# Sample columns of the expert outputs from gathered rows, and the last group in token halves

## The reference, cut to what matters

```
qh = (xb @ w_pq).reshape(..., 8 heads, 2, 128)
s = qh . sub_keys                             # 128 scores for each half and head
sv, si = top_k(s, 16)                         # of each half
cand = sv[half 0][:, None] + sv[half 1][None, :];  top_s, pos = top_k(cand, 16)
eid = si[half 0] * 128 + si[half 1]           # at pos: 16 of 16384 experts for each head
gate = softmax(top_s)
act = gelu(u_experts[eid] . xb)
out = sum over the 8 * 16 (gate * act) * v_experts[eid]
x = x + out;   y = rmsnorm(x) * norm_final
```

## Time and profile before

| | |
|---|---|
| median of 3 runs | 5116.29 us |
| profiled execution | 5119.69 us, span 5117.5 us |
| TensorE / VectorE / ScalarE / GpSimd busy | 98% / 48% / 24% / 24% |
| mean granted TensorE clock | 0.988 of 2.4 GHz |
| HBM traffic | 539 MB read, 111 MB written, 127 GB/s |

### The profile page before, as it was taken

How to read it: one execution, slowest core, us unless ns; L and a number is a source line. 1 busy time by engine, 2 the same in 40 slices (tenths; PEclk the granted TensorE clock), 3 DMA queues, 4 the chain that set the end, 5 groups by cost and what they waited for, 6 DMA issues and landing times. The chain is left out here.

```text
span 5117.5 us, 92582 instructions
## 1 busy us (share of the span) xinstructions
PE 5005.5 (98%) x39028; PEld 4930.2 (96%) x39028; DVE 2452.4 (48%) x3709; ACT 1231.9 (24%) x1251; POOL 1206.5 (24%) x522
## 2 busy tenths in 40 slices
PE   8999999999989999999999999999999999999997
PEld 8999888899969999999999999999999999999997
DVE  4455556533222335765777776501444444444443
ACT  4233334222121222222111111122212212212212
POOL 0000000020001003333333333334223233233232
PEclk9999999899989999999999999999999999999998
DMA  3233433232342234333444344443333333333332
GB/s 150 96 130 119 153 105 108 93 121 90 132 149 86 95 108 164 120 120 106 137 132 150 133 153 137 153 165 144 135 138 128 135 135 129 138 131 129 141 125 76
DMA packets 233944, 651.28 MB, mean 127 GB/s; under 512 B 13696, under 2 KB 126720, under 8 KB 177024
## 3 DMA queue, kind: packets, MB, share of 16 engines
q1 hardware_dynamic: 233856, 650.03, 36.0%
HBM read 539.42 MB, written 110.56 MB: 127 GB/s over the span
## 5 line engine op out<-in xcount | busy, mean ns | idle before, releaser
L237 PE MATMUL pu<-xhi,whi 128*128 128x272 f32 x7456 | 1548.0, 289 | 28.6 <-DVE xlo L503 12.5
L237 PE MATMUL pu<-xhi,wlo 128*128 128x272 f32 x7456 | 1545.9, 289 | 0.0
L237 PE MATMUL pu<-xlo,whi 128*128 128x272 f32 x7456 | 1540.7, 288 | 0.0
L237 PEld LDWEIGHTS pu<-xhi,whi 128*128 128x128 f32 x7456 | 1174.4, 189 | 31.5 <-issue 24.3
L237 PEld LDWEIGHTS pu<-xlo,whi 128*128 128x128 f32 x7456 | 1175.2, 189 | 0.0
L237 PEld LDWEIGHTS pu<-xhi,wlo 128*128 128x128 f32 x7456 | 1167.2, 189 | 0.0
L221 ACT CAST whi<-raw 128x2048 fp32r<-128x2048 f32 x393 | 748.5, 1905 | 1593.3 <-PE pm L237 1183.5
L226 POOL TENSOR_TENSOR wlo<-raw,whi 128x2048 fp32r<-128x2048 f32 x128 | 601.5, 4699 | 1210.1 <-ACT whi L221 1210.1
L226 DVE TENSOR_TENSOR wlo<-raw,whi 128x2048 fp32r<-128x2048 f32 x265 | 609.4, 2300 | 390.9 <-ACT whi L221 383.9
L1492 POOL TENSOR_TENSOR clo<-coef,chi 128x544 fp32r<-128x544 f32 x124 | 261.6, 2130 | 994.3 <-ACT chi L1496 994.3
L1556 DVE TENSOR_TENSOR x<-pm,x 128x544 f32<-128x544 f32 x256 | 185.5, 724 | 584.1 <-PE pm L237 584.1
(11 more groups left out here) (298 smaller groups left out, 4796.4 us busy)
## 6 DMA issues: line engine op xcount, KB each, us to landing
raw<-units SPq DMA_DIRECT2D x393, 1024.0 KB, 4.9
h_s<-h_out SPq DMA_DIRECT2D x128, 272.0 KB, 2.1
gate_s<-table SPq DMA_DIRECT2D x17, 2048.0 KB, 9.4
h_in<-h_s SPq DMA_DIRECT2D x32, 1088.0 KB, 7.1
gate_in<-gate_s SPq DMA_DIRECT2D x32, 1088.0 KB, 9.1
q_s<-q_out SPq DMA_DIRECT2D x32, 320.0 KB, 2.2
x<-xT SPq DMA_DIRECT2D x8, 1088.0 KB, 6.7
qh<-q_s SPq DMA_DIRECT2D x8, 1088.0 KB, 7.3
```

Of the source, the lines that this page charges most:

```text
L237: ins = nc.tensor.matmul(out, w, xs[b][m == 1], start=(first and n == 0 and m == 0), stop=(last and n == len(terms) - 1 and m == 2))
```

## The change

- **Sample tokens.** The output stage no longer carries the 32 sample columns: `chi`, `clo`, `coef`, `h_in`, `gate_in` and the table have 512 columns (`TP`), and a product has one operand of 512 columns in one bank instead of two of 272. The table has 16 chunks; the transposes and copies of the fifth token block go.
- **Slots.** In the fifth block the 96 empty tokens become three copies of the 32 sample tokens (`again`), so that its 128 partitions hold each token four times. Partition group g keeps 32 of the token's 128 slots (`dve_keep_slots`): a gate, the address of the h value in `h_s`, and the address of the expert's weight row in `units`.
- **Gathers.** In the output stage GpSimd issues for each of the 32 slots one indirect DMA for 128 values of h and 16 for 128 rows of 512 bytes (`pool_rows`), behind the coefficient steps of `pair_pool`: one slot in a group, two in groups 0, 6, 12, 18 and 24, done by group 26. Three buffers. Two groups later VectorE multiplies h by the gate and adds h * gate * row to `row_sum` (`dve_row`).
- **Sample result.** Ahead of the last pair TensorE multiplies `row_sum` by a selection matrix (`pe_sample`: 16 products, which sum the four copies and turn the result), and VectorE adds it to `x` (`dve_sample`).
- **Last group.** Its 512 columns are done as two halves of 256 tokens one after the other, with its four units loaded and split a second time. The norm of the first half (sum, root, scaling, stores) stands between the units of the second; the `Norm` block goes. The 32 sample columns go with the second half. The scaled tiles have a buffer each and are stored two at a time.

The core of the diff:

```diff
+    def dve_keep_slots(chain):
...
+        for g in range(P // TS):
+            ps, cs = slice(TS * g, TS * (g + 1)), slice(SLOTS * g, SLOTS * (g + 1))
+            v.tensor_copy(row[ps], flat(row_key)[ps, cs])
+            v.tensor_copy(col[ps], flat(col_key)[ps, cs])
+            ins = v.tensor_copy(slot_gate[ps], flat(gate)[ps, cs])
...
+    slots_of = lambda group: range(min(group + (group + 5) // 6, SLOTS), min(group + 1 + (group + 6) // 6, SLOTS)) if group >= 0 else ()
+    def pool_rows(pool, group):
+        for j in slots_of(group):
+            s = j % 3
+            if j >= 3:
+                pool.wait_ge(row_used, j - 2)
+            nc.gpsimd.indirect_dma_start(slot_h[:, j:j + 1], None, h_s.rearrange("k p (t o) -> (k p t) o", o=1),
+                                         bass.IndirectOffsetOnAxis(ap=slot_at[:, j:j + 1], axis=0)).then_inc(row_loaded[s], 16)
+            for o in range(KT):
+                nc.gpsimd.indirect_dma_start(rows[s][:, o], None, a["units"].rearrange("u p (t n) -> (u p t) n", n=P),
+                                             bass.IndirectOffsetOnAxis(ap=slot_row[:, j:j + 1], axis=0),
+                                             element_offset=o // 4 * (P * KT * P) + o % 4 * (GRP * P)).then_inc(row_loaded[s], 16)
+    def dve_row(dve, j):
+        s = j % 3
+        dve.wait_ge(row_loaded[s], 16 * (KT + 1) * (j // 3 + 1))
+        nc.vector.tensor_tensor(slot_h[:, j:j + 1], slot_h[:, j:j + 1], slot_gate[:, j:j + 1], ALU.mult).then_inc(slots_kept, 1)
...
+            ins = nc.vector.scalar_tensor_tensor(row_sum[:], rows[s][:], slot_h[:, j:j + 1], row_sum[:], ALU.mult, ALU.add)
+    def pe_sample(pe):
+        pe.wait_ge(row_used, SLOTS)
+        for k in range(KT):
+            ins = nc.tensor.matmul(pm[:, 0, 1, k * TS:(k + 1) * TS], row_sum[:, k], consts[:, C_SEL:C_SEL + TS], start=True, stop=True)
...
-                    products([out_slot(d)[:, b, 0:HALF] for b in (0, 1)],
-                             [(whi[:, slot, GRP * d + k], wlo[:, slot, GRP * d + k], halves(chi[r], clo[r], k)) for k in range(GRP)],
+            products([out_slot(d)[:, 0, cols]],
+                     [(whi[:, slot, GRP * d + k], wlo[:, slot, GRP * d + k], [(chi[r][:, k, cols], clo[r][:, k, cols])]) for k in range(GRP)],
...
+                unit_pe(pe, i, r, VU * r + w, PART[0] if last and r else slice(0, TP), w == 0)
+    PART = [slice(0, TP // 2), slice(TP // 2, TP)]
+    WIDTH = [slice(0, TP // 2), slice(TP // 2, T)]
...
     def pair_dve(dve, i, last):
         for n in range(2 * VU):
+            if n % 2 == 0:
+                for j in slots_of(2 * i + n // VU - 2)[n % VU // 2:n % VU // 2 + 1]:
+                    dve_row(dve, j)
...
     def pair_pool(pool, i, last):
         pool_coefs(pool, i * 2 + 1, 1, i + 1)
+        pool_rows(pool, 2 * i)
         if not last:
             pool_coefs(pool, i * 2 + 2, 0, i + 2)
+            pool_rows(pool, 2 * i + 1)
...
+        with pe.Fori(0, END) as i:
+            pair_pe(pe, i, False)
+        pe_sample(pe)
+        pair_pe(pe, END, True)
+        for w in range(VU):
+            unit_pe(pe, END, 1, 2 * VU + w, PART[1])
+            if w == 0:
+                total(0)
+        total(1)
...
+        for w in range(VU):
+            if w < VU - 1:
+                ahead_act(act, END, 2 * VU + w)
+            if w == 1:
+                root(act, 0)
+            squares_of(act, 1, range(4 * w, 4 * w + 4))
+        root(act, 1)
```

More of the change, by code:

```diff
@@ L326, in build @@
     counts["squares"] += KT
[L328 to L361, removed]
     place = region(WR, W_SIZE)
@@ L1157, in build @@
     ROUTED = NCH * STRETCH
-    TCH = T // TC
+    TCH = TP // TC
     CHUNK_UNITS = 4
@@ L1424, in hidden_stage_tensor, with stretch @@
     def hidden_stage_tensor(pe):
-        with pe.Fori(0, NCH) as t:
+        def stretch(t, turned):
             def between(m, n):
@@ L1435, in hidden_stage_tensor @@
                 hidden_pe(pe, 0, STRETCH, t, m, before=lambda n: between(m, n))
+        with pe.Fori(0, NCH - 1) as t:
+            stretch(t, True)
+        stretch(NCH - 1, False)
         with pe.Fori(0, TCH) as c:
@@ L1479, in build @@
     place = region(HR, H_SIZE)
-    chi = [place(f"chi{i}", [GRP, T], F32R) for i in (0, 1)]
-    clo = [place(f"clo{i}", [GRP, T], F32R) for i in (0, 1)]
+    chi = [place(f"chi{i}", [GRP, TP], F32R) for i in (0, 1)]
+    clo = [place(f"clo{i}", [GRP, TP], F32R) for i in (0, 1)]
+    rows = [place(f"rows{i}", [KT, P]) for i in range(3)]
+    row_sum = place("row_sum", [KT, P])
+    slots_of = lambda group: range(min(group + (group + 5) // 6, SLOTS), min(group + 1 + (group + 6) // 6, SLOTS)) if group >= 0 else ()
@@ L1506, in pair_sp @@
                 m = VU * r + w
-                if not (last and m >= 2 * VU - 2):
-                    load_unit(sp, i * (2 * VU) + (V0 + m + 2), (V0 + m) % 2)
+                load_unit(sp, i * (2 * VU) + (V0 + m + 2), (V0 + m) % 2, UNITS - 3 * VU + m + 2 if last and m >= 2 * VU - 2 else None)
                 if (r, w) == (0, 0):
@@ L1514, in pair_sp, with unit_pe, operand_ready @@
                     load_group(sp, i * 2 + (r + 2), r)
-    def pair_pe(pe, i):
+        if last:
+            for w in range(VU - 2):
+                load_unit(sp, UNITS + w + 2, (V0 + w) % 2, UNITS - VU + w + 2)
+    def unit_pe(pe, i, r, n, cols, first=False):
+        slot = (V0 + n) % 2
+        pe.wait_ge(lo_ready, i * (2 * VU) + (V0 + n + 1))
+        def operand_ready(k):
+            pe.wait_ge(clo_ready, i * (2 * GRP) + (GRP * r + k + 1))
+        for d in range(4):
+            if d % 2 == 0:
+                pe.wait_ge(psum_free, i * (2 * KT) + (V0 + 4 * n + d))
+            products([out_slot(d)[:, 0, cols]],
+                     [(whi[:, slot, GRP * d + k], wlo[:, slot, GRP * d + k], [(chi[r][:, k, cols], clo[r][:, k, cols])]) for k in range(GRP)],
+                     before=operand_ready if first and d == 0 else None).then_inc(tiles_done, 1)
@@ L1517, in pair_pe @@
+    def pair_pe(pe, i, last):
         for r in (0, 1):
             for w in range(VU):
[L1519 to L1528, removed]
-                    products([out_slot(d)[:, b, 0:HALF] for b in (0, 1)],
-                             [(whi[:, slot, GRP * d + k], wlo[:, slot, GRP * d + k], halves(chi[r], clo[r], k)) for k in range(GRP)],
-                             before=operand_ready if (w, d) == (0, 0) else None).then_inc(tiles_done, 1)
+                unit_pe(pe, i, r, VU * r + w, PART[0] if last and r else slice(0, TP), w == 0)
@@ L1536, in pair_act @@
                 n = VU * r + w
-                if not (last and n == 2 * VU - 1):
-                    split_hi(act, (V0 + n + 1) % 2, i * VU + ((V0 + n + 1) // 2 + 1), i * (2 * KT) + (V0 + 4 * n))
+                ahead_act(act, i, n)
                 if w < 2 and not (last and r):
@@ L1562, in pair_pool @@
         else:
             pool.wait_ge(clo_ready, NGRP * GRP)
-            sum_tiles(pool, T, squares_before)
+            clear_sum(pool)
+            for b in (0, 1):
+                for k in range(KT):
+                    at = squares_before + KT * b + k
+                    pool.wait_ge(squared, at + 1)
+                    pool.wait_ge(squares_summed, at + PRIME)
+                    nc.gpsimd.tensor_tensor(sumsq[:, WIDTH[b]], sumsq[:, WIDTH[b]], squares[:, k % 2, 0:WIDTH[b].stop - WIDTH[b].start], ALU.add).then_inc(squares_summed, 1)
```

169 lines of the change are left out of this document (125 added, 44 removed).

## The result

The changed kernel takes 5075.84 us (median of four runs, 5072.72 to 5083.78), the one before 5114.31 in the same comparison: a ratio of 0.9926, interval 0.9909 to 0.9943. So 38 us are gained where 136 were forecast; That is 0.7%, clear of noise. 5075.84 lies inside the range, close to its upper end, and 96 us above the predicted time. The profiled execution took 5076.88 us, its span is 5075.1.

The account below looks back on a forecast made before the run. TensorE's columns were taken to bound the output stage. Terms -128 - 4 + 6 - 10 = -136 us from 5119.7 gave 4984, or 4980 against the median of 5116.3; the range was 4960 to 5080.

Parts of the forecast that it names:

- What bounds it: Output stage: TensorE, busy for all of a 48.10 us group, sets the pace by columns times instructions.
- 512 columns: Output stage: one 512-column product at 0.229 us replaces two of 272; 44.0 us a group, 128 us gained over 31.
- Table, sample's products: Gate table loses one chunk, 3.8 us gained; at the end, sample products add 5.6 us on the path.
- The sample's rows: Output stage: 544 indirect DMAs, each holding GpSimd 1.0 us, cost nothing; up to 1.15 us each nothing is late.
- rival 1: GpSimd becomes a bound in the five double stretches, at 1.15 to 1.7 us per DMA; typically 5040 us; chance 0.27.
- 34c - 39: TensorE's stop in us per double stretch: 34 gathers at c us of GpSimd each, against 39 us of room.
- the rival on the other side: Gathers above about 1.75 us each set the pace of 27 of 32 groups; 5260 us at 2.0; chance 0.14.
- hidden: Output stage: VectorE's multiply-add per slot fits within the 11 us of a unit; uncovered it would be 83 us.
- The last group: Last group in halves plus end: 68 us instead of 77.5, a gain of 10 us.
- the ring of cast, subtraction, adds and squares: Last group: this loop around a half unit takes 6.4 us with handovers, against 5.7 us on TensorE.
- 13 or so: End, behind the last half unit: sum, totals, root, scalings and store take about 13 us with handovers.

Follow-up runs that it names:

- gates first: Changed kernel, with GpSimd lowering due coefficients and making the following group's gates, one group earlier than before, before issuing gathers; everything computed: 4972.59 us.
- twelve gathers a slot: Changed kernel with 12 of the 16 weight gathers of each slot, leaving out the last 512 of 2048 values: 4999.68 us.
- the run without doubles: Changed kernel without the last 5 of 32 slots, so one slot a group and no stretch with 34 gathers: 4988.85 us.
- one gather a slot: Changed kernel with each slot's 128 weight rows fetched by one gather of 8 KB rows from a natural-layout weight copy: 4971.20 us.

## Why the prediction was wrong

**What bounds it, and 512 columns: right.** TensorE's columns set the pace of every group that nothing disturbs. ScalarE's casts of two units, 12.03 us apart in the earlier trace rows, now stand like this:

```profile
3573.84 1.92 ACT L225 CAST whi<-raw 128x2048 fp32r<-128x2048 f32 x1 [8.96 <-PE pm L241]
3584.72 1.92 ACT L225 CAST whi<-raw 128x2048 fp32r<-128x2048 f32 x1 [8.96 <-PE pm L241]
```

10.88 us for 48 steps are 0.2267 each, where the earlier trace rows gave 0.229; inside the 0.225 to 0.233 named as the test. 0.0023 us less on 5952 steps (14), and a group before at 48.16 instead of 48.1 (2), make the gain 144 and not 128. Without the gathers' loss the forecast would have been too slow: the run with the gates first stands at 4972.59 against the 4980 predicted.

**Table, sample's products: right in size.** -7.8 against -4 is within what the start of the stage varies from run to run. The sample's products cost 3.6 instead of 6: their 32 records took 3.65 us, 0.11 each instead of 0.175.

**The sample's rows: the step that failed**, "I take 1.0 us" for what an indirect DMA holds GpSimd, and with it "At 1.0 us: nothing". Rows of GpSimd after the change (start, us; in brackets idle before), and one of VectorE, give it:

```profile
3564.08 0.94 POOL L1510 DMA_INDIRECT rows<-units,gcum  x1 [0.30 <-issue]
3565.33 2.68 POOL L1510 DMA_INDIRECT rows<-units,gcum  x1 [0.30 <-issue]
3568.31 0.94 POOL L1510 DMA_INDIRECT rows<-units,gcum  x1 [0.30 <-issue]
...
3564.90 2.29 DVE L230 TENSOR_TENSOR wlo<-raw,whi 128x2048 fp32r<-128x2048 f32 x1 [1.25 <-ACT whi L225]
```

1.25 us from one to the next, and 2.98 where a subtraction of VectorE stands beside it (3564.90 to 3567.19). The first double stretch took 47.1 us for 34, 1.39 each, past the 1.15 up to which nothing is late. So rival 1 came out: its place (five doubles) and its chain (coefficient cast, weight cast, subtraction) were right. Its threshold was too high: twelve gathers a slot were late at 37.1 us. And its price was too low. By 34c - 39 a double costs 8 us, 41 in all, and the time would have been 5021. The first double cost 18.5, and three things that the price left out make the difference: the subtraction stands still beside GpSimd's late gates and lowerings (7.49 us for 2.29, +5.2); TensorE comes back at half clock (8.15 us for 5.44, +2.7); and the next stretch is late too (+2.0), its chain being VectorE's small product, which stands still for the same reason:

```profile
3645.45 7.09 DVE beta L1517
...
3657.31 5.76 PE pu L241 x24
```

8.1 + 5.2 is 13.3 of the 13.8 us of the wait. By the starts of TensorE's products, against 10.88 us a unit, the other four doubles cost 19.0 to 19.4 each: 12.5 us of wait, some 2 at the lower clock, 4.7 in the next stretch, where TensorE waits for 2.8 us and then has a mean granted clock of 0.59 for 4 us (3938.7 to 3942.7). That is 95 us for the doubles. Of the other stretches 13 lose 0.6 to 1.9 us, 12 together, and the first unit of the stage loses 1.8, as it does without gathers: 109 in all. That doubles make 90 and the rest 19 is shown by the run without doubles as well; the pieces of a double are read from the trace and not each taken away in a run of their own.

That the measured time still lies in the range is luck: the range reached up to c = 1.7 by a price that was too low, and c was 1.39.

For the rival on the other side I had an end of 2.1 us, where a DMA lands. It did not come out: with one gather a slot, a gather of 4-byte values lands 2.6 us after its issue and holds GpSimd for 0.98.

```profile
beta<-h_s,egcum POOLq DMA_INDIRECT x32, 2.6
```

The Trainium skill, page "DMA: Bandwidth & Descriptors", section Anatomy of one DMA, puts most of its 2.0 us behind the issue. These two numbers agree with that.

**The words "hidden" for VectorE's 2.3 us a slot: half right.** Where the row work stands beside GpSimd's gathers it is hidden (gates first: TensorE waits for nothing in the stretch of 256 us shown). Beside GpSimd's gates it, or the subtraction behind it, takes three times as long (6.89 us for 2.35, 7.96 for 2.29). That the two engines stop each other was in no step. The Trainium skill, page "SBUF — State Buffer", section Who interferes with whom, says that a VectorE instruction with two inputs from that memory contends with a GpSimd instruction that reads it, for a pair of ports that works as an exclusive lock. The runs agree and go further: VectorE waited for a whole run of GpSimd's instructions (the rest of one gate, another gate and two lowerings for the product of 4.74 us), not for one.

**The last group: wrong in size, and my own terms did not add up.** The half unit was put at 6.4 us, the ring of cast, subtraction, adds and squares; it took 7.13 because the squares wait for GpSimd's sums through two buffers. With four it is 6.39. Eight took 57.3 us (forecast 55). Behind the last product stand 16.7 us; the terms that I listed, 2 + 1 + 2.2 + 7.2 + 2.6, make 15, not "13 or so". The end of TensorE's part, against the earlier trace rows:

```profile
5058.27 0.28 PE L241 MATMUL pm<-chi,wlo 128*128 128x256 f32 x1
5061.90 0.87 PE L1682 MATMUL pu<-sumsq,consts 128*128 128x288 f32 x2 [3.35 <-POOL sumsq L1662]
```

Add, square and sum take 3.4 instead of 2. The group of the scalings, against the first of the earlier trace rows:

```profile
L1634 DVE SCALAR_TENSOR_TENSOR y_out<-x,vecs,rinv 128x288 f32<-128x288 f32 (+1 forms) x20 | 9.5, 544 | 3.9 <-ACT rinv L1612 3.9
```

The 6.3 us of waiting for stores of before are gone, as forecast. The step's real gap is elsewhere: I compared the halves with the end of before and not with a whole group at the new width. The halves save 5 us behind the last product (16.7 for 21.7) and cost 13.8 in front of it (57.3 for 43.5).

## What to carry to other kernels

Price an added instruction not by its engine's idle share but by what stands behind it in that engine's line: the same gathers cost 109 us in one order and 2 us at most in another, and moving the work that is due soon ahead of the work that isn't was the whole repair. Where an engine's slack is a threshold, put the doubled stretches against it and not the mean, and add to an overrun what a stalled TensorE loses in clock and what VectorE loses beside GpSimd. Splitting a last group to overlap its tail pays only if a half costs half; here eight half units took 57.3 us where four whole ones take 43.5.

## What was not expected of the hardware

- An indirect DMA of 128 rows holds GpSimd for 0.94 us, with 0.30 idle before the next, whether a row has 4 B, 512 B or 8 KB (0.98, 0.94, 0.94).
- VectorE and GpSimd stop each other: VectorE's 128x1 product took 0.15 us beside GpSimd's gathers and 4.74 beside its gates, the subtraction 2.29 and 7.96; a gather took 2.68 beside a subtraction. VectorE's adds with an operand in PSUM kept their 0.69 us.
- After a wait of 13.8 us TensorE's granted clock was 0.50 for 4 us, and back at 1.00 8.2 us after its start (between them 0.86): 2.7 us lost on top of the wait.
